# Units and sums of the feed-forward at a different offset in their slots for each pair

## The chip, the cores and the metric

The kernel runs on one core of one Trainium2 chip. The metric is the device time of one execution in microseconds; the kernel before has a median of 2101.1 us over three runs (2100.09 to 2101.67).

## What is computed

One layer of a diffusion backbone over 512 tokens of width 2048 (with 256 context tokens): a mixer, half Fourier transform and half gated linear recurrence, and then a feed-forward with a short convolution. All is in float32. The change touches the feed-forward alone, which takes more than half of the time:

```python
def conv_ffn(h, w_up, conv_w, conv_b, w_down):
    up = depthwise_conv(h @ w_up, conv_w, conv_b, FFN_CONV // 2)
    g, v = jnp.split(up, 2, axis=-1)
    return (jax.nn.gelu(g, approximate=True) * v) @ w_down

hx2 = modulate(rms_norm(x, g_ffn_pre[l]), sh2, sc2)
x = x + gt2 * rms_norm(conv_ffn(hx2, w_up[l], conv_ffn_w[l], conv_ffn_b[l], w_down[l]), g_ffn_post[l])
```

The width inside is 5632, that is 44 tiles of 128 features each for the gate g and for the value v.

## The kernel before

**Three matmuls for one product.** A float32 matrix is split into a rounded part (hi) and the rest (lo). `three` (lines 994 to 998) makes a product of 128 x 128 weights and up to 512 tokens as hi x hi (line 996), hi weights x lo data (997) and lo weights x hi data (998). Each matmul loads its own weights.

**Units.** All weights come as a stream of units of 128 x 1024 elements (`UNIT`, 8 blocks of 128 x 128). SyncE loads unit n into slot `SLOT[n]` of `w_raw` (line 471), a ring of 5 slots whose rows are `PITCH` = 1088 elements apart, so 64 elements of a slot are spare. ScalarE rounds it into the same slot of `w_hi` (lines 606 and 610); VectorE subtracts and writes `w_lo` in place of `w_raw` (lines 1536 and 1540: `twice` gives both names the same bytes). TensorE waits for `lo_done` and counts the unit as used at its last matmul; that lets SyncE load the unit four later.

**The feed-forward.** A pair is one tile of g and one of v. It has four units. In chunks of 4 pairs (`c` from 0 to 10, `p` from 0 to 3) the loops run over the pairs; after the first pair of a chunk stands the down projection of the chunk before, 8 units with 192 matmuls of 512 columns. From chunk 1 on (40 pairs) `up_pair` takes a pair in this order:
- `four_tiles` on the first unit `u`: 24 matmuls of 512 columns (8 blocks, three each);
- `seven_products` on `u + 1` and `u + 2`: the second half of the input features by a scheme with seven products instead of eight, on half the tokens. Each unit gives 8 blocks as they are and 6 blocks of sums, three matmuls each, 42 matmuls of 256 columns: 84 for both;
- `four_tiles` on the last unit `u + 3`: 24 matmuls of 512 columns.

The sums of blocks are made by VectorE (`sum_blocks`, lines 2029 to 2048) as soon as the raw unit has landed, then rounded and split as the unit is (lines 608 and 1538). `WSUM` names the units with sums: those of `u + 1` lie in the fifth slot of the ring (`SUMS0`), those of `u + 2` in `sums1_raw`, `sums1_hi` and `sums1_lo`.

**Where a block starts.** `ASIDE` = 16 elements (64 bytes): units of `WSUM` and all sums start 64 bytes into their slot (`at_slot`, `sums_of`), all other units at its first byte. Tensors named `gap_...` hold no data; they set where the next tensor begins. The streamed data are `h_hi`, `h_lo` (the input), `t_hi`, `t_lo` (sums of the input, made once) and `act_hi`, `act_lo` (the activations, for the down projection). The last four units of all (`KEPT`) are in h_hi and h_lo, without an offset.

**What sets the order.** Each engine runs its own list, written out by hand; semaphores tie them together. Nothing in the order depends on where a block lies.

Of the kernel before, what the change touches and what calls it, by code (L numbers as in the profile page):

```python
# [8 lines left out]
F32R = mybir.dt.float32r  # L9
ALU = mybir.AluOpType  # L10
ACT = mybir.ActivationFunctionType
ds = bass.ds

P = 128
# [9 lines left out]
CH = 4  # L24
NCH = FT // CH
UNIT = 8 * P
# [8 lines left out]
for _h in range(2, 8):  # L35
    _n = SLOT0 + 4 * (_h - 2)
# [10 lines left out]
UP, DOWN = {}, {}  # L47
_n = OUT_H[KT - 1][1] + 1
# [12 lines left out]
UNITS = _n + KT // 2  # L61
# [8 lines left out]
WSUM = {}  # L70
# [1 line left out]
    for _p in range(CH):  # L72
        WSUM[UP[_c, _p] + 1], WSUM[UP[_c, _p] + 2] = 0, 1
NSUM = 3 * 2 * P
ASIDE = 16

SLOT, BEFORE, TURN = [], [], []
for _n in range(UNITS):
# [3 lines left out]
SUMS0 = R0 % RING  # L82
# [85 lines left out]
def build(nc, x1_d, x_t, ctx_t, par_d, late_d, stream, ada0, adabg, gates_d, tabs_d, wf_d, out_t):  # L168
    ctx = ExitStack()
    with ctx:  # L170
# [3 lines left out]
        def sbuf(stack, name, shape, dt=F32, side=None):  # L174
            return stack.enter_context(nc.sbuf_tensor(name, shape, dt, side=side))

        def twice(stack, raw, name, shape):

            with ExitStack() as s:
                first = sbuf(s, raw, shape)  # L180
            return first, sbuf(stack, name, shape, F32R)
# [12 lines left out]
        w_raw, w_lo = twice(ctx, "w_raw", "w_lo", [P, RING, PITCH])  # L194
        w_hi = sbuf(ctx, "w_hi", [P, RING, PITCH], F32R)
# [67 lines left out]
        fin = ExitStack()  # L263
# [3 lines left out]
        t_raw, t_lo = twice(fin, "t_raw", "t_lo", [P, 4, 3 * H])  # L267
        t_hi = sbuf(fin, "t_hi", [P, 4, 3 * H], F32R)
        up_sum = sbuf(fin, "up_sum", [P, 2 * L])
        sbuf(fin, "gap_to_sums", [P, ASIDE])  # L270
        sums1_raw, sums1_lo = twice(fin, "sums1_raw", "sums1_lo", [P, NSUM])
        sbuf(fin, "gap_to_x1", [P, 256 - ASIDE])
        acc = sbuf(fin, "acc", [P, KT * L])
        with ExitStack() as s:
            late_par = sbuf(s, "late_par", [P, NLATE])
# [6 lines left out]
        mixer.close()  # L282
        with ExitStack() as s:
            sbuf(s, "late_kept", [P, NCONV])
            sbuf(s, "gap_to_sums_hi", [P, 32 + ASIDE])
            sums1_hi = sbuf(s, "sums1_hi", [P, NSUM], F32R)
            cg = sbuf(s, "cg", [P, 2, L])
            cv = sbuf(s, "cv", [P, L])
            sbuf(s, "gap_to_act", [P, 416 - 32 - ASIDE])
            act_hi = sbuf(s, "act_hi", [P, CH, L], F32R)  # L290
            act_lo = sbuf(s, "act_lo", [P, CH, L], F32R)
        ss2 = up_sum[:, 0:L]
        ss_last = up_sum[:, L:2 * L]
        fin.close()

        def at_slot(n):

            return ds(ASIDE if n in WSUM else 0, UNIT)

        def raw_unit(n):  # L300
            if n < UNITS - KEPT:
                return w_raw[:, SLOT[n], at_slot(n)]
            i = n - UNITS + KEPT
            return x0[:, 2 * i:2 * i + 2, :].rearrange("p k l -> p (k l)")

        def hi_unit(n):
            if n < UNITS - KEPT:
                return w_hi[:, SLOT[n], at_slot(n)]
            i = n - UNITS + KEPT
            return h_hi[:, 2 * i:2 * i + 2, :].rearrange("p k l -> p (k l)")  # L310

        def lo_unit(n):
            if n < UNITS - KEPT:
                return w_lo[:, SLOT[n], at_slot(n)]
            i = n - UNITS + KEPT
            return h_lo[:, 2 * i:2 * i + 2, :].rearrange("p k l -> p (k l)")

        def sums_of(n):

            if WSUM[n]:  # L320
                return sums1_raw[:, :], sums1_hi[:, :], sums1_lo[:, :]
            return tuple(w[:, SUMS0, ds(ASIDE, NSUM)] for w in (w_raw, w_hi, w_lo))

        def x1_back(k):

# [139 lines left out]
        def _(sp):  # L465
            def load_unit(n):
                if n >= UNITS - KEPT:
                    sp.wait_ge(*used(DOWN[NCH - 1] - 1))
                elif BEFORE[n] >= 0:
                    sp.wait_ge(*used(BEFORE[n]))  # L470
                sp.dma_start(raw_unit(n), stream[n]).then_inc(raw_sem(n)[0], 16)
# [125 lines left out]
        def _(act):  # L597
# [3 lines left out]
            def hi(*units):  # L601
                for n in units:
                    act.wait_ge(*raw_sem(n))
                    if n in WSUM:
                        act.wait_ge(blocks_summed, sum(u <= n for u in WSUM))
                        a.activation(hi_unit(n), raw_unit(n), ACT.Copy)  # L606
                        raw, high, _ = sums_of(n)
                        a.activation(high, raw, ACT.Copy).then_inc(hi_done, 1)
                    else:
                        a.activation(hi_unit(n), raw_unit(n), ACT.Copy).then_inc(hi_done, 1)  # L610
# [380 lines left out]
        def _(pe):  # L991
# [8 lines left out]
            def block_of(n, j):  # L1000
                return hi_unit(n)[:, P * j:P * j + P], lo_unit(n)[:, P * j:P * j + P]
# [375 lines left out]
            def seven_products(n, w, b):  # L1377

                alone_g, alone_v, common, parts = (bank[i] for i in b)
                pe.wait_ge(lo_done, n + 1)  # L1380
                _, high, low = sums_of(n)

                def product(out, block, x, start, stop):
# [144 lines left out]
        def _(dve):  # L1528
# [3 lines left out]
            def lo(*units):  # L1532
                for n in units:
                    dve.wait_ge(hi_done, n + 1)
                    if n in WSUM:
                        v.tensor_tensor(lo_unit(n), raw_unit(n), hi_unit(n).bitcast(F32), ALU.subtract)  # L1536
                        raw, high, low = sums_of(n)
                        v.tensor_tensor(low, raw, high.bitcast(F32), ALU.subtract).then_inc(lo_done, 1)
                    else:
                        v.tensor_tensor(lo_unit(n), raw_unit(n), hi_unit(n).bitcast(F32), ALU.subtract).then_inc(lo_done, 1)  # L1540
# [782 lines left out]
```

## Time and profile before

| | |
|---|---|
| median of 3 runs | 2101.1 us |
| the profiled execution | 2102.9 us |
| its span, first to last instruction | 2101.1 us |
| TensorE matmul busy | 2066.7 us, 98% |
| TensorE weight load busy | 1767.6 us |
| VectorE busy | 1529.7 us, 73% |
| ScalarE busy | 812.0 us, 39% |
| DMA, mean over the span | 148 GB/s |

Busy time of a matmul runs from its start to the end of its last column's way through the array, so matmuls that follow one another overlap in it: one of 512 columns shows 389 ns and the next starts 227 ns after it. The spacing of two starts is what a matmul costs in a full stream; it is read from the start times of the timeline.

### The profile page before, as it was taken

Reading aid. Unit: us, or ns where it says so; the run is one execution under the profiler, and the core shown is the slowest. Engines: PE = TensorE matmul, PEld = TensorE weight load, DVE = VectorE, ACT = ScalarE, POOL = GpSimd, SP = SyncE. Lnnn points to the kernel's source line nnn. Section 1 sums busy time; section 2 is a strip of 40 time slices with the busy share of each in tenths; the row PEclk is TensorE's granted clock in tenths of the full one; section 3 lists DMA queues with packets and bytes.
Section 4 is the critical chain, followed back from the end, with each engine's and each line's share of the span. In section 5 each row is a group of like instructions: output and inputs, shape, how many; then the busy total and the mean of one; then the engine's idle time right before and its main releaser. Section 6 shows DMA issues by size and latency. Waiting matters only on the chain.

```text
span 2101.1 us, 28297 instructions
## 1 busy us (share of the span) xinstructions
PE 2066.7 (98%) x11682; PEld 1767.6 (84%) x11682; DVE 1529.7 (73%) x2202; ACT 812.0 (39%) x1077; POOL 79.0 (4%) x145
## 2 busy tenths in 40 slices
PE   7999999999999999999999999999999999999998
PEld 4678887888777888888889898898988888888887
DVE  5567978876979886767767676676776768577577
ACT  5347576543323352423324243242333324233243
POOL 0000000001110000000000000000000000000002
PEclk9999999999999999999999999999999999999999
DMA  9953424434876524333333333434333333233342
GB/s 394 408 205 111 156 93 163 136 110 169 322 269 230 181 90 140 101 121 119 104 131 104 124 112 109 131 101 140 101 120 121 101 126 101 95 101 101 100 179 103
DMA packets 86193, 311.19 MB, mean 148 GB/s; under 512 B 9456, under 2 KB 13552, under 8 KB 84016
## 3 DMA queue, kind: packets, MB, share of 16 engines
q1 hardware_dynamic: 67824, 243.09, 33.3%
q0 software_dynamic: 17424, 65.50, 9.4%
q8 instruction: 92, 1.51, 0.3%
q10 hardware_dynamic: 816, 0.79, 0.1%
q14 instruction: 37, 0.30, 0.1%
HBM read 300.95 MB, written 8.39 MB: 147 GB/s over the span
## 4 chain that ended last, share of the span: by engine, by line
PE 68%; DVE 2%; DMA 1%; issue 1%; ACT 0%; DVEq 0%; ACTq 0%
PE bank L996 23%; PE bank L998 22%; PE bank L997 22%; DMA ada_raw<-in_adabg 1%; DVE w_lo L1540 1%; DVE acc L2175 0%; PE bank L1107 0%; DVE ada_acc L1572 0%; PE bank L1321 0%; DMA w_raw<-in_stream 0%; DVE x L1880 0%; DVE prod L1891 0%; ACT w_hi L610 0%; DVE ss L1548 0%; PE bank L1292 0%
## 5 line engine op out<-in xcount | busy, mean ns | idle before, releaser
L996 PE MATMUL bank<-h_hi,w_hi 128*128 128x512 f32 (+1 forms) x1968 | 711.1, 361 | 5.9 <-ACT acc L855 2.0
L997 PE MATMUL bank<-h_lo,w_hi 128*128 128x512 f32 (+1 forms) x1968 | 708.1, 360 | 0.0
L998 PE MATMUL bank<-h_hi,w_lo 128*128 128x512 f32 (+1 forms) x1968 | 706.5, 359 | 0.0
L1540 DVE TENSOR_TENSOR w_lo<-w_raw,w_hi 128x1024 fp32r<-128x1024 f32 x260 | 316.0, 1222 | 159.4 <-ACT w_hi L610 159.1
L996 PEld LDWEIGHTS bank<-h_hi,w_hi 128*128 128x128 f32 x1968 | 370.4, 188 | 65.5 <-issue 11.0
L610 ACT ACTIVATE w_hi<-w_raw 128x1024 fp32r<-128x1024 f32 x260 | 273.2, 1056 | 388.6 <-DMA w_raw<-in_stream 388.6
L998 PEld LDWEIGHTS bank<-h_hi,w_lo 128*128 128x128 f32 x1968 | 370.2, 188 | 56.8
L997 PEld LDWEIGHTS bank<-h_lo,w_hi 128*128 128x128 f32 x1968 | 372.8, 189 | 49.0
L996 PE MATMUL bank<-act_hi,w_hi 128*128 128x512 f32 (+1 forms) x688 | 265.0, 385 | 1.9 <-DVE acc L2147 1.5
L997 PE MATMUL bank<-act_lo,w_hi 128*128 128x512 f32 (+1 forms) x688 | 264.3, 384 | 0.0
L998 PE MATMUL bank<-act_hi,w_lo 128*128 128x512 f32 (+1 forms) x688 | 264.2, 384 | 0.0
L606 ACT ACTIVATE w_hi<-w_raw 128x1024 fp32r<-128x1024 f32 x80 | 85.0, 1062 | 335.9 <-DVE w_raw L2048 335.9
L2075 DVE TENSOR_TENSOR acc<-acc,bank 128x512 f32<-128x512 f32 x144 | 98.3, 687 | 134.6 <-PE bank L998 134.4
L996 PEld LDWEIGHTS bank<-act_hi,w_hi 128*128 128x128 f32 x688 | 129.2, 188 | 28.1 <-DVE h_lo L1540 1.9
L997 PEld LDWEIGHTS bank<-act_lo,w_hi 128*128 128x128 f32 x688 | 129.3, 188 | 25.7
L998 PEld LDWEIGHTS bank<-act_hi,w_lo 128*128 128x128 f32 x688 | 129.3, 188 | 25.6
L1572 DVE SCALAR_TENSOR_TENSOR ada_acc<-ada_raw,csil,ada_acc 128x1024 f32<-128x1024 f32 x105 | 134.5, 1281 | 10.8 <-DMA ada_raw<-in_adabg 6.5
L558 POOL DMA_DIRECT2D ada_raw<-in_adabg x112 | 59.8, 534 | 1537.3 <-DVE ada_acc L1572 1135.2
L1536 DVE TENSOR_TENSOR w_lo<-w_raw,w_hi 128x1024 fp32r<-128x1024 f32 x80 | 97.4, 1217 | 0.0
L996 PE MATMUL bank<-t_hi,w_hi 128*128 128x256 f32 x320 | 89.9, 281 | 0.0
L997 PE MATMUL bank<-t_lo,w_hi 128*128 128x256 f32 x320 | 89.9, 281 | 0.0
L998 PE MATMUL bank<-t_hi,w_lo 128*128 128x256 f32 x320 | 89.9, 281 | 0.0
(340 smaller groups left out, 2707.8 us busy)
## 6 DMA issues: line engine op xcount, KB each, us to landing
w_raw<-in_stream SPq DMA_DIRECT2D x340, 512.0 KB, 3.5
ada_raw<-in_adabg POOLq DMA_DIRECT2D x112, 512.0 KB, 4.7
ada_raw<-in_ada SPq DMA_DIRECT2D x64, 512.0 KB, 13.6
x<-in_x_t SPq DMA_DIRECT2D x4, 1024.0 KB, 8.4
acc<-in_adabg SPq DMA_DIRECT2D x8, 512.0 KB, 6.3
x<-in_x_t POOLq DMA_DIRECT2D x4, 1024.0 KB, 9.0
x_kept_d<-x SPq DMA_DIRECT2D x4, 1024.0 KB, 5.6
c<-in_ctx_t SPq DMA_DIRECT2D x2, 1024.0 KB, 14.1
```

Of the source, the lines that this page charges most:

```text
L558: pool.dma_start(ada_raw(slot), adabg[COLS[q // KT] * KT + q % KT]).then_inc(ada_in[slot], 16)
L606: a.activation(hi_unit(n), raw_unit(n), ACT.Copy)
L610: a.activation(hi_unit(n), raw_unit(n), ACT.Copy).then_inc(hi_done, 1)
L996: t.matmul(out, w, v, start=start, stop=False)
L997: t.matmul(out, w, v_l, start=False, stop=False)
L998: return t.matmul(out, w_l, v, start=False, stop=stop)
L1536: v.tensor_tensor(lo_unit(n), raw_unit(n), hi_unit(n).bitcast(F32), ALU.subtract)
L1540: v.tensor_tensor(lo_unit(n), raw_unit(n), hi_unit(n).bitcast(F32), ALU.subtract).then_inc(lo_done, 1)
L1572: v.scalar_tensor_tensor(dst, ada_raw(s), scale, dst, ALU.mult, ALU.add).then_inc(ada_eaten, 1)
L2075: v.tensor_tensor(tile(acc, m), tile(acc, m), bank[4 + m % 4][:, :], ALU.add).then_inc(down_added, 1)
```

## The change

It makes the offset a table by unit, with one entry for the hi copy (`HI_ASIDE`) and one for the raw and lo copies (`LO_ASIDE`), in elements of 4 bytes. Pairs are counted from chunk 1 on (`_n` from 0 to 39). The first unit, the two middle units and their sums get another offset in each pair; the last unit, the down projection and everything ahead of chunk 1 stay at 0. In bytes, with s = 16 x (`_n` mod 16):

| pairs | first unit hi, lo | middle units and sums hi, lo |
|---|---|---|
| 0 to 15 | s, s | s, s |
| 16 to 31 | 0, s | 64, s |
| 32 to 39 | 2s + 8, 2s + 8 | 0, 2s + 16 |

The tensors for the second sums grow by 64 elements and the gaps beside them shrink, so that all else stays where it was.

```diff
-ASIDE = 16
+HI_ASIDE, LO_ASIDE = [0] * UNITS, [0] * UNITS
+for _c in range(1, NCH):
+    for _p in range(CH):
+        _n, _u = (_c - 1) * CH + _p, UP[_c, _p]
+        _step = 4 * (_n % 16)
+        if _n < 16:
+            _first, _seven = (_step, _step), (_step, _step)
+        elif _n < 32:
+            _first, _seven = (0, _step), (16, _step)
+        else:
+            _first, _seven = (2 * _step + 2, 2 * _step + 2), (0, 2 * _step + 4)
+        HI_ASIDE[_u], LO_ASIDE[_u] = _first
+        for _i in (1, 2):
+            HI_ASIDE[_u + _i], LO_ASIDE[_u + _i] = _seven
...
-        sbuf(fin, "gap_to_sums", [P, ASIDE])
-        sums1_raw, sums1_lo = twice(fin, "sums1_raw", "sums1_lo", [P, NSUM])
-        sbuf(fin, "gap_to_x1", [P, 256 - ASIDE])
+        sums1_raw, sums1_lo = twice(fin, "sums1_raw", "sums1_lo", [P, NSUM + 64])
+        sbuf(fin, "gap_to_x1", [P, 256 - 64])
...
-            sbuf(s, "gap_to_sums_hi", [P, 32 + ASIDE])
-            sums1_hi = sbuf(s, "sums1_hi", [P, NSUM], F32R)
+            sbuf(s, "gap_to_sums_hi", [P, 32])
+            sums1_hi = sbuf(s, "sums1_hi", [P, NSUM + 64], F32R)
...
-            sbuf(s, "gap_to_act", [P, 416 - 32 - ASIDE])
+            sbuf(s, "gap_to_act", [P, 416 - 32 - 64])
...
-        def at_slot(n):
-
-            return ds(ASIDE if n in WSUM else 0, UNIT)
-
...
-                return w_raw[:, SLOT[n], at_slot(n)]
+                return w_raw[:, SLOT[n], ds(LO_ASIDE[n], UNIT)]
...
-                return w_hi[:, SLOT[n], at_slot(n)]
+                return w_hi[:, SLOT[n], ds(HI_ASIDE[n], UNIT)]
...
-                return w_lo[:, SLOT[n], at_slot(n)]
+                return w_lo[:, SLOT[n], ds(LO_ASIDE[n], UNIT)]
...
+            high, low = ds(HI_ASIDE[n], NSUM), ds(LO_ASIDE[n], NSUM)
             if WSUM[n]:
-                return sums1_raw[:, :], sums1_hi[:, :], sums1_lo[:, :]
-            return tuple(w[:, SUMS0, ds(ASIDE, NSUM)] for w in (w_raw, w_hi, w_lo))
+                return sums1_raw[:, low], sums1_hi[:, high], sums1_lo[:, low]
+            return w_raw[:, SUMS0, low], w_hi[:, SUMS0, high], w_lo[:, SUMS0, low]
```

## Rows read from the trace of the kernel before

**Rows 1.** The page: busy time, share, instructions; granted clock by slice.
```profile
PE 2066.7 (98%) x11682; PEld 1767.6 (84%) x11682; DVE 1529.7 (73%) x2202; ACT 812.0 (39%) x1077; POOL 79.0 (4%) x145
...
PEclk9999999999999999999999999999999999999999
```

**Rows 2.** The page: the chain that ended last, by engine and by line.
```profile
PE 68%; DVE 2%; DMA 1%; issue 1%; ACT 0%; DVEq 0%; ACTq 0%
PE bank L996 23%; PE bank L998 22%; PE bank L997 22%; DMA ada_raw<-in_adabg 1%; DVE w_lo L1540 1%; DVE acc L2175 0%; PE bank L1107 0%; DVE ada_acc L1572 0%; PE bank L1321 0%; DMA w_raw<-in_stream 0%; DVE x L1880 0%; DVE prod L1891 0%; ACT w_hi L610 0%; DVE ss L1548 0%; PE bank L1292 0%
```

**Rows 3.** Waits of PE, 905 to 2060 us: total us, times, longest.
```profile
PE bank L996 <- DVE acc L2147: 1.9, 3, 0.9
PE bank L996 <- DVE act_lo L1988: 0.4, 1, 0.4
```

**Rows 4.** Timeline of PE, one pair: start us, duration us; first unit, then middle.
```profile
1356.46 0.39 PE L996 MATMUL bank<-h_hi,w_hi 128*128 128x512 f32 x1
...
1361.67 0.39 PE L998 MATMUL bank<-h_hi,w_lo 128*128 128x512 f32 x1
1361.89 0.28 PE L996 MATMUL bank<-h_hi,w_hi 128*128 128x256 f32 x1
```

**Rows 5.** The same timeline: last middle matmul, then the last unit.
```profile
1371.67 0.28 PE L998 MATMUL bank<-t_hi,sums_lo 128*128 128x256 f32 x1
1371.79 0.40 PE L996 MATMUL bank<-h_hi,w_hi 128*128 128x512 f32 x1
...
1372.49 0.40 PE L996 MATMUL bank<-h_hi,w_hi 128*128 128x512 f32 x1
...
1373.18 0.39 PE L996 MATMUL bank<-h_hi,w_hi 128*128 128x512 f32 x1
...
1377.26 0.39 PE L996 MATMUL bank<-h_hi,w_hi 128*128 128x512 f32 x1
```

**Rows 6.** Timeline of PE, last down projection, weights from h_hi and h_lo.
```profile
2071.78 0.28 PE L996 MATMUL bank<-act_hi,h_hi 128*128 128x256 f32 x1
...
2072.74 0.28 PE L998 MATMUL bank<-act_hi,h_lo 128*128 128x256 f32 x1
```

**Rows 7.** Timeline of PE, Fourier stage, weights from eo_hi and eo_lo.
```profile
417.87 0.29 PE L998 MATMUL bank<-m_hi,eo_lo 128*128 128x256 f32 x1
...
419.06 0.28 PE L996 MATMUL bank<-m_hi,eo_hi 128*128 128x256 f32 x1
```

**Rows 8.** Timeline of PE, mixer: 256 columns after 512, and 512 after 256.
```profile
179.02 0.28 PE L996 MATMUL bank<-hc_hi,w_hi 128*128 128x256 f32 x1
179.13 0.28 PE L997 MATMUL bank<-hc_lo,w_hi 128*128 128x256 f32 x1
...
179.37 0.40 PE L996 MATMUL bank<-xc_hi,g_hi 128*128 128x512 f32 x1
...
180.07 0.40 PE L996 MATMUL bank<-xc_hi,g_hi 128*128 128x512 f32 x1
```

**Rows 9.** Groups of VectorE, 905 to 2060 us: count, busy us, mean ns, idle before.
```profile
L1540 DVE TENSOR_TENSOR w_lo<-w_raw,w_hi 128x1024 fp32r<-128x1024 f32 x145 | 177.4, 1223 | 117.0 <-ACT w_hi L610 116.9
L1536 DVE TENSOR_TENSOR w_lo<-w_raw,w_hi 128x1024 fp32r<-128x1024 f32 x70 | 85.2, 1217 | 0.0
```

**Rows 10.** Timeline, all engines: a first middle unit made ready, and its first matmul.
```profile
1082.97 0.95 DVE L1538 TENSOR_TENSOR w_lo<-w_raw,w_hi 128x768 fp32r<-128x768 f32 x1
...
1085.81 0.28 PE L996 MATMUL bank<-h_hi,w_hi 128*128 128x256 f32 x1
```

**Rows 11.** Loads of units, 1000 to 2000 us: least, median, longest.
```profile
DMA to landing us min/median/max: 3.3/3.5/5.9
```

**Rows 12.** Waits of VectorE for a landed unit, 1000 to 2000 us: total, times, longest.
```profile
DVE w_raw L2043 <- DMA w_raw<-in_stream: 17.6, 13, 2.3
```

## The prediction

> **What bounds the kernel now.** I read four views in this order. First the page's busy times and its slices: the matmul array is busy 2066.7 of 2101.1 us, VectorE 1529.7 and ScalarE 812.0, with the granted clock of its slices at nine tenths or more throughout [rows 1]. Then the chain that ended last: 67 of its 68 percentage points on PE are the three matmul lines 996 to 998 [rows 2]. Then the waits of PE over the feed-forward (905 to 2060 us): 2.3 us in all, most of it in the last down projection [rows 3]. So within the pairs no weight unit is late, and the kernel is as long as the sum of the spacings from one matmul start to the next. What the change can move directly is that spacing; everything else works only by making a unit late.
>
> The reader is to see that the spacing is not the columns alone. In the first unit of a pair 24 matmuls of 512 columns start in 5.43 us, 226 to 227 ns each [rows 4]; in the two middle units 84 of 256 columns start from 1361.89 to 1371.79 us, 117.8 ns each [rows 4, 5]. In the last down projection, where matmuls of 256 columns take weights from h_hi and h_lo with no offset, eight start in 0.96 us, 120.0 ns each [rows 6]. The gap tensors of lines 215 to 291 and the slot pitch put every tensor that the feed-forward's matmuls stream, and every slot that they load, at one remainder of 128 bytes (worked out from the sizes in the allocations). So 120.0 ns belongs to an offset of 0, 117.8 to one of 64 bytes. A third point: in the Fourier stage moving data (m_hi, m_lo) and weights (eo_hi, eo_lo) are 32 bytes apart by the same count, and ten spacings take 417.87 to 419.06 us, 119.0 ns each [rows 7]. The offset of the weights against the streamed data therefore costs or gives about 2 ns a matmul, and these three points are all that the trace has.
>
> For 512 columns there is only offset 0. But there is the return to it: of the first six matmuls of the last unit, after the 84, three take 0.70 us (1371.79 to 1372.49, 233 ns each) and three 0.69 (to 1373.18, 230 ns), and only then do 18 of them take 4.08 us (to 1377.26, 226.7 ns each) [rows 5]. The even 227 is a state that the stream settles into, and off it the array is slower here.
>
> **The change, part by part.** No instruction is added, removed or moved, and no wait. What changes is the start of a block in its slot. Of 40 pairs from the second chunk on:
> - The first unit (24 matmuls of 512 columns) leaves offset 0 by a remainder of 128 bytes in 14 of the first 16 pairs, for w_lo alone in 14 of the next 16, and by 8 bytes and more in the last 8: 36 pairs.
> - The middle units and sums (84 of 256) leave 64 bytes. In the first 16 pairs both copies walk in steps of 16 bytes: 2 pairs at 64, 2 at 0, 12 between. In the next 16 w_hi stays at 64 and w_lo walks: 14 pairs. In the last 8 w_hi is at 0 and w_lo between.
> - The last unit and the down projection stay at 0.
>
> *Middle units.* An offset of 0 costs 120.0 - 117.8 = 2.2 ns, one between 119.0 - 117.8 = 1.2 ns (the Fourier point, the nearest row). First 16 pairs: 84 x (2 x 2.2 + 12 x 1.2) = 1.6 us. Next 16: one load in three is moved; I take half of 1.2, since the three share one stream: 84 x 14 x 0.6 = 0.7 us. Last 8: two loads at 0 and one between, 1.9 ns: 84 x 8 x 1.9 = 1.3 us. Sum 3.6 us. Bounds: single spacings of 0.11 us occur, but as the first of 256 columns after three of 512 (179.02 to 179.13 us), repaid by three of 512 in 0.70 us right after (179.37 to 180.07) [rows 8]; no row holds under 117.8. For the end below I take 1.2 ns gained, the same size as the loss between: 36 x 84 x 1.2 = 3.6 us off. For the end above, 2.2 ns everywhere: 6.7 us.
>
> *First unit.* If an offset keeps the stream from its settled state, 230.0 - 226.7 = 3.3 ns, the second three above; 36 x 24 x 3.3 = 2.9 us. Ends: 2.2 ns gained, as 64 bytes gives in the middle units, 1.9 us off; and 6.6 ns lost, the first three's 233.3, 5.7 us.
>
> *Crossings.* Each pair now pays 1.39 - 6 x 0.2267 = 0.03 us once on returning to the last unit [rows 5]. New crossings stand where a shifted first unit follows the last one; I take half of that, 36 x 0.015 = 0.5 us, with 0 and 1.0 as ends.
>
> *Off the path.* DMAs, ScalarE's roundings and VectorE's subtractions now write and read at 16 or 8 bytes. VectorE already does it at two offsets: 1223 ns at 0 (line 1540) and 1217 at 64 bytes (line 1536) [rows 9]; 6 ns by 160 instructions is 1 us of an engine with 570 us to spare. The cover is the lead of the units: the tightest is the first middle unit, whose w_lo is ready at 1082.97 + 0.95 = 1083.92 us and first used at 1085.81 [rows 10], 1.9 us early. Unit loads land 3.3 to 5.9 us after issue, median 3.5 [rows 11]. So I cost all this at nothing; below nothing is excluded, as no wait of PE is there to shorten.
>
> Sum: 3.6 + 2.9 + 0.5 = 7.0 us. The profiled execution took 2102.9 us with a span of 2101.1, against a median of 2101.1; the terms are differences, so they go on the median: 2101.1 + 7.0 = 2108.1 us.
>
> **A rule that speaks against this working.** The rows show 120.0 and 117.8 ns for the same 256 columns [rows 4 to 6]. The Trainium skill (SBUF — State Buffer, Who interferes with whom) gives TensorE two independent read ports, one for streamed data and one for weights, and says that it never waits on anyone; by that an offset could cost nothing, and the trace does not agree, unless the 2.2 ns comes from something else that differs in the tail. This is the second rival. The same page (its box on cachelines) has lines of 16 bytes; by that only the first units of the last 8 pairs, which start 8 bytes into a line, would differ.
>
> **Rivals.**
> 1. *Slower, by late units.* A load whose rows begin on a 16-byte or 8-byte multiple may land later. For it: sum_blocks already waits for landings [rows 12]; against: both offsets of before land alike, but both are multiples of 32 bytes within one 64. The point from which it decides is 1.9 us more per landing, over half of the median 3.5. If landings doubled, the first middle unit would be 3.5 - 1.9 = 1.6 us late in the 24 pairs whose raw block starts off a multiple of 32 bytes: 38 us at worst, and with half of them 19: about 2120. The Trainium skill (Collectives: The Full Stack, Rules for kernel authors) asks for 32-byte alignment to prevent a read-modify-write; no run here shows one.
> 2. *No change, by independence.* The middle units' 117.8 against 120.0 is due to act_hi as moving data or to h_hi as weights, not to 64 bytes; or each stream settles at the same spacing whatever the offset, only shifted in time. For it: streams of offset 0 do return to 227 from any start within six matmuls. Against: the Fourier point between the two. Price: 0 to 2 us, 2101 to 2103.
> 3. *Slower at the upper ends.* 6.7 + 5.7 + 1.0 = 13.4 us: 2114.5. Beyond it, should the untried offsets be as much worse than 0 as 0 is worse than 64 bytes, another 6.7 us: 2121.
> 4. *Faster, by the lower ends.* The conflict is smallest somewhere between: 3.6 + 1.9 = 5.5 us off, 2095.6. For it: 0 was never the best where another was seen. Against: the 64 bytes of now is the best of three points.
>
> **How the numbers follow.** Forecast (offsets cost about what the three points say, 2105 to 2112) 0.45; rival 2, 0.27; rival 3, 0.12; rival 4, 0.12; rival 1, 0.04. A measurement of this kernel can tell about 0.2% (4.2 us) from no change, so "slower" begins at 2105.3: nearly all of the forecast less 0.02, rivals 3 and 1, together 0.59. "Same": rival 2 and 0.02 of the forecast, with 0.02 of rival 4: 0.31. "Faster": 0.10. The range leaves out rival 1, half of rival 3 above 2115 and most of rival 4 below 2098: 2098 to 2115.
>
> **What would show it.** In the trace of after: spacings of the 84 middle matmuls pair by pair, 117.8 in the pairs whose offset is 64 or 192 bytes and 119 to 120 elsewhere; spacings of the first unit above 227 in 36 pairs; the last unit still with its 0.03 us; PE's waits still near 2 us. It is wrong if first units stay at 227 at any offset (rival 2), if a row of an offset lies far off 117 to 120, or if PE waits for VectorE at line 996 (rival 1).

## The result and the profile after

The changed kernel takes 2106.5 us (median of 10 runs) beside 2101.5 for the kernel before (10 runs on the same chip): 1.0021 times as long over all runs, 95% interval 1.0013 to 1.0029: a small loss, clear of no change. The forecast was 2108.1 us, with a range of 2098 to 2115. The profiled execution has a span of 2105.8 us, 4.7 more than before.

The waits and the engines other than TensorE are as they were; the matmul array is busy 7 us more, and recorded busy times overlap. First a line of the page of the changed kernel (busy time, share, instructions), then the waits of PE from 905 to 2065 us, then what the loads of units took to land from 900 to 2060 us (least, median, longest):

```profile
PE 2073.7 (98%) x11682; PEld 1769.5 (84%) x11682; DVE 1530.1 (73%) x2202; ACT 811.9 (39%) x1077; POOL 78.7 (4%) x145
```

```profile
PE bank L1005 <- DVE acc L2156: 1.9, 3, 0.8
PE bank L1005 <- DVE act_lo L1997: 0.3, 1, 0.3
```

```profile
DMA to landing us min/median/max: 3.3/3.5/5.6
```

PE waits 2.2 us where it waited 2.3 [rows 3], the loads land in 3.5 us in the median, as in [rows 11], and the 66 of the 215 that begin off a multiple of 32 bytes do so too (3.3 us at least, 5.0 at most), and VectorE's time is 0.4 us more. So the 4.7 us lie in the spacings of the matmuls. Summed from one start to the next over all 40 pairs, first units take 4.1 us more, middle units 0.4, last units 0.2, the down projections nothing: 4.7 (4.65 before rounding).

The timeline of PE shows where (start us, duration us; each time the first matmul of a unit). Pair 1, first unit at 16 bytes, 24 matmuls from 827.25 us on; pair 2, at 32 bytes, from 848.10 on:

```profile
827.25 0.39 PE L1005 MATMUL bank<-h_hi,w_hi 128*128 128x512 f32 x1
...
832.69 0.28 PE L1005 MATMUL bank<-h_hi,w_hi 128*128 128x256 f32 x1
...
848.10 0.39 PE L1005 MATMUL bank<-h_hi,w_hi 128*128 128x512 f32 x1
...
853.69 0.28 PE L1005 MATMUL bank<-h_hi,w_hi 128*128 128x256 f32 x1
```

5.44 us are 226.7 ns a matmul, as at 0 bytes in [rows 4]; 5.59 us are 232.9. (The lines are rounded to 0.01 us, which is 0.4 ns a matmul here; the table below is made from the unrounded starts.) Then the 84 middle matmuls of pair 4 and of pair 20. Both have them at 64 bytes in both copies, as all pairs had before:

```profile
895.75 0.28 PE L1005 MATMUL bank<-h_hi,w_hi 128*128 128x256 f32 x1
...
905.65 0.40 PE L1005 MATMUL bank<-h_hi,w_hi 128*128 128x512 f32 x1
...
1406.64 0.28 PE L1005 MATMUL bank<-h_hi,w_hi 128*128 128x256 f32 x1
...
1416.16 0.40 PE L1005 MATMUL bank<-h_hi,w_hi 128*128 128x512 f32 x1
```

9.90 us are 117.8 ns a matmul, 9.52 us are 113.3. The same offsets, the same work, two speeds: nothing in the prediction has room for this. By the table of offsets the two pairs differ in the first unit ahead, at (64, 64) in pair 4 and (0, 64) in pair 20.

Since each pair of the changed kernel has its own offsets, its trace can be laid out as a table, each value seen once and behind its own neighbours. Mean spacing in ns over the unit, from the start times of the timeline (offsets in bytes, hi and lo copy; s as in the table of the change):

| s | first unit (s, s) | first unit (0, s) | middle (s, s) | middle (64, s) |
|---|---|---|---|---|
| 0 | 226.7 | 226.7 | 119.9 | 117.8 |
| 16 | 226.7 | 226.7 | 118.3 | 117.8 |
| 32 | 233.1 | 233.1 | 118.4 | 117.8 |
| 48 | 233.3 | 231.9 | 118.3 | 116.7 |
| 64 | 233.3 | 230.9 | 117.8 | 113.4 |
| 80 | 231.9 | 231.5 | 118.8 | 117.8 |
| 96 | 234.2 | 232.1 | 118.7 | 118.8 |
| 112 | 233.3 | 233.0 | 119.9 | 118.6 |
| 128 | 232.7 | 231.1 | 118.8 | 118.2 |
| 144 | 226.7 | 226.7 | 119.8 | 117.8 |
| 160 | 233.3 | 233.0 | 119.9 | 117.9 |
| 176 | 230.0 | 230.8 | 118.1 | 117.0 |
| 192 | 228.9 | 231.1 | 117.8 | 113.6 |
| 208 | 231.8 | 230.8 | 116.6 | 117.8 |
| 224 | 233.3 | 231.4 | 116.6 | 117.0 |
| 240 | 226.7 | 226.7 | 117.3 | 117.7 |

In the last eight pairs the first units (8 to 232 bytes in steps of 32) run at 226.7 to 233.7 ns, with 226.7 at 40 bytes, the middle ones at 117.8 to 118.9. So first units know one good rhythm, 226.7 ns, which they have at 0, 16, 40, 144 and 240 bytes, and else run 2 to 8 ns above it, never below. The two middle streams at 113.4 and 113.6 ns have one rhythm, three spacings of 113, 113 and 114 ns over and over, 113.3 in the mean; the rest is the first one or four spacings, which are longer.

### The profile page after: what moved, and what is told of

It reads as the page before. It is cut to its first block, busy times and chain, and to the rows that moved or that the text cites. A ratio compares the mean times of both kernels' runs of the same rounds, so it can differ in the third digit from the quotient of the medians.

```text
span 2105.8 us, 28297 instructions
## 1 busy us (share of the span) xinstructions
PE 2073.7 (98%) x11682; PEld 1769.5 (84%) x11682; DVE 1530.1 (73%) x2202; ACT 811.9 (39%) x1077; POOL 78.7 (4%) x145
## 4 chain that ended last, share of the span: by engine, by line
PE 69%; DVE 2%; DMA 1%; issue 0%; ACT 0%; DVEq 0%; ACTq 0%
PE bank L1005 23%; PE bank L1007 23%; PE bank L1006 23%; DMA ada_raw<-in_adabg 0%; DVE acc L2184 0%; DVE w_lo L1549 0%; PE bank L1116 0%; PE bank L1325 0%; DMA w_raw<-in_stream 0%; ACT h_hi L619 0%; DVE ada_acc L1581 0%; DVE x L1889 0%; PE bank L1330 0%; PE bank L1301 0%; DVE acc L2156 0%
## 5 line engine op out<-in xcount | busy, mean ns | idle before, releaser
L1545 DVE TENSOR_TENSOR w_lo<-w_raw,w_hi 128x1024 fp32r<-128x1024 f32 x80 | 97.5, 1219 | 0.0
```

## The experiments

Two theories stood against each other. **H**: a stream of matmuls settles into a rhythm, and which one depends on the offsets and on the state in which the stream is entered. **F**: each offset has a price of its own. Each experiment keeps all instructions of the changed kernel and alters only the table of offsets, unless its edit says more. In the edits `...` stands for lines left out, `OFFSETS` lists for each pair the bytes of the first unit (hi, lo) and of the middle units (hi, lo), and `HI_ASIDE` and `LO_ASIDE` count elements of 4 bytes (16 is 64 bytes, 48 is 192).

**First units alone.** The offsets of the changed kernel for first units, 64 bytes for all middle units and sums.

```diff
+OFFSETS = (
+    (0, 0, 64, 64), (16, 16, 64, 64), (32, 32, 64, 64), (48, 48, 64, 64),
...
-        HI_ASIDE[_u], LO_ASIDE[_u] = _first
...
+        _fh, _fl, _sh, _sl = (_x // 4 for _x in OFFSETS[(_c - 1) * CH + _p])
+        HI_ASIDE[_u], LO_ASIDE[_u] = _fh, _fl
...
-            HI_ASIDE[_u + _i], LO_ASIDE[_u + _i] = _seven
+            HI_ASIDE[_u + _i], LO_ASIDE[_u + _i] = _sh, _sl
```

> The first units' offsets of the changed kernel in all 40 pairs, the middle units and sums at 64 bytes as before. Theory H (a stream of matmuls settles into a rhythm, and which one depends on how it is entered as well as on the offset): first units add the 4.1 us that the changed trace shows for them, and pair 20 (first unit 0 and 64 bytes) runs its 84 middle matmuls at 113.4 ns as it did there; the middle units together lose nothing or gain 0.4 us or more; in all 3.3 to 4.1 us slower. Rival F (each offset has one price of its own): first units plus 4.1 us, middle units 117.8 ns in every pair, in all 4.1 us slower.

Measured: 2100.6 us beside 2102.1, ratio 0.9993 (0.9983 to 1.0003), no change that the runs can tell. In the trace first units cost 4.07 us more than before, as forecast, and middle units 5.13 us less, which neither theory had: with all middle units at (64, 64), 26 pairs run them at 117.8 ns and 14 pairs at 113.3 to 113.6, those whose first unit is at (128, 128), (160, 160), (176, 176), (0, 32), (0, 64), (0, 80), (0, 96), (0, 112), (0, 128), (0, 176), (0, 224), (104, 104), (136, 136) or (200, 200). The recorded durations go with the spacings, 276 ns where the stream has 113.3 and 281 where it has 117.8; they are no second witness, as the end of a matmul is modelled in the profile. Least, median and longest of the matmuls on the second sums, 905 to 2060 us (before they are all 281 ns):

```profile
L1012 PE MATMUL bank<-t_lo,sums_hi x142: 276/281/281, 904.8 to 2027.1; 128*128 128x256 f32 x142
```

Equal offsets, two rhythms and nothing between: F falls. H had the mechanism and not its reach; it named pair 20 alone, and its 3.3 to 4.1 us slower stand against 1.1 us less in the spacings.

**Middle units alone.** First units at 0, middle units and sums as in the changed kernel.

```diff
+OFFSETS = (
+    (0, 0, 0, 0), (0, 0, 16, 16), (0, 0, 32, 32), (0, 0, 48, 48),
...
-        HI_ASIDE[_u], LO_ASIDE[_u] = _first
...
+        HI_ASIDE[_u], LO_ASIDE[_u] = _fh, _fl
```

> The middle units' and sums' offsets of the changed kernel, the first units at 0 as before. Theory H: pairs 20 and 28 (64, 64 and 64, 192 bytes), which ran at 113.4 and 113.6 ns in the changed kernel, fall to about 117.8 when entered from a first unit at 0, so the middle units cost 0.4 + 0.7 = 1.1 us. Rival F: they keep the changed kernel's spacings, pair 20 at 113.4 too, 0.4 us in all.

Measured: 2104.1 us beside 2102.1, ratio 1.0006 (0.9996 to 1.0015), no change that the runs can tell. The trace gives middle units 0.92 us more than before. Pair 20, at (64, 64), and pair 28, at (64, 192), timeline of PE:

```profile
1406.02 0.28 PE L1011 MATMUL bank<-h_hi,w_hi 128*128 128x256 f32 x1
...
1415.91 0.40 PE L1011 MATMUL bank<-h_hi,w_hi 128*128 128x512 f32 x1
...
1659.60 0.28 PE L1011 MATMUL bank<-h_hi,w_hi 128*128 128x256 f32 x1
...
1669.13 0.40 PE L1011 MATMUL bank<-h_hi,w_hi 128*128 128x512 f32 x1
```

Pair 20 has fallen back to 117.7 ns (117.8 from the unrounded starts), as H expects; pair 28 has not, 113.5 ns. So (64, 64) depends on the entry, and (64, 192) may not. Other values of the table hang on the entry too: behind a first unit at 0, (96, 96) runs at 117.4 ns where the changed kernel had 118.7, and (128, 128) at 120.1 where it had 118.8.

**Every pair as pair 20.**

```diff
+        HI_ASIDE[_u], LO_ASIDE[_u] = 0, 16
...
+            HI_ASIDE[_u + _i], LO_ASIDE[_u + _i] = 16, 16
```

> Every pair as pair 20 of the changed kernel: first unit 0 (hi) and 64 (lo) bytes, middle units and sums 64 and 64. Theory H: 84 x (117.8 - 113.4) = 0.37 us gained and 24 x (231.0 - 226.7) = 0.10 us lost in each pair, 40 x 0.27 = 10.7 us faster than before, about 2090.7. Rival F (the offsets 64 and 64 are worth 117.8, as before, and pair 20 was a single occurrence): 4.1 us slower, about 2105.5.

Measured: 2093.0 us beside 2102.1, ratio 0.9956 (0.9939 to 0.9974), that is 9.2 us faster. In the trace middle units take 14.7 us less than before and first units 4.1 more, 10.6 us in all, against 10.7 expected. One pair, first unit, middle units and the first matmul of the last unit:

```profile
888.55 0.39 PE L998 MATMUL bank<-h_hi,w_hi 128*128 128x512 f32 x1
...
894.10 0.28 PE L998 MATMUL bank<-h_hi,w_hi 128*128 128x256 f32 x1
...
903.62 0.40 PE L998 MATMUL bank<-h_hi,w_hi 128*128 128x512 f32 x1
```

5.55 us instead of 5.43, 9.52 instead of 9.90. All 40 pairs show these times within 0.01 us, though VectorE is busy in 28% of the middle units' time in one pair and in 85% in another, and ScalarE in 11% to 47%: the work beside it does not set the spacing. Middle units keep the offset of before here, so all that they gain comes from what stands ahead of them.

**Twenty entries, two kinds of middle units.** Pairs 0 to 19 at (64, 64), pairs 20 to 39 at (64, 192), each behind the same 20 first units.

```diff
+OFFSETS = (
+    (0, 0, 64, 64), (16, 16, 64, 64), (144, 144, 64, 64), (240, 240, 64, 64),
...
+        HI_ASIDE[_u], LO_ASIDE[_u] = _fh, _fl
...
+            HI_ASIDE[_u + _i], LO_ASIDE[_u + _i] = _sh, _sl
```

> One look at 20 different first units (both copies from 0, 16, 40, 64, 144, 192, 240 bytes), each followed by middle units at 64, 64 (pairs 0 to 19) and at 64, 192 bytes (pairs 20 to 39). Theory H: among equal middle units some run at 117.8 and some at 113.4 to 113.6 ns, with (0, 64) in pair 17 and (0, 192) in pair 38 at about 113.5; where a first unit keeps 226.7 ns and the middle ones run at 113.5, 0.36 us a pair are to be had for nothing. Rival F: all of pairs 0 to 19 alike, all of 20 to 39 alike, within 0.2 ns.

Measured, a single execution (2097.1 us), so only its trace is read: at (64, 64) only the entry from (0, 64) leads to 113.4 ns. The 17 first units that themselves keep 226.7 ns, such as (16, 16), (40, 40) or (144, 240), all lead to 117.8, and so do (0, 192) and (64, 0). At (64, 192) all 20 entries lead to 113.4 to 113.6 ns over the 84, that is to the rhythm of 113.3 after one to five spacings, also those from a first unit at 0 (pair 20 of this kernel):

```profile
1404.37 0.28 PE L1011 MATMUL bank<-h_hi,w_hi 128*128 128x256 f32 x1
...
1413.91 0.40 PE L1011 MATMUL bank<-h_hi,w_hi 128*128 128x512 f32 x1
```

9.54 us, 0.36 less than in [rows 4, 5], and the first unit loses nothing.

**All middle units at 64 and 192 bytes.** First units at 0.

```diff
+        HI_ASIDE[_u], LO_ASIDE[_u] = 0, 0
...
+            HI_ASIDE[_u + _i], LO_ASIDE[_u + _i] = 16, 48
```

> First units at 0 as before; middle units and sums with the hi copy at 64 and the lo copy at 192 bytes in all 40 pairs. Theory H (a stream settles into a rhythm; at 64, 192 all 20 entries tried led to 113.3 ns, at 64, 64 only some): 84 x (117.8 - 113.3) less the first matmuls = 0.353 us in each pair, 14.1 us faster than before, about 2088. Rival G (the trace's spacings overstate: what the middle units gain comes back later, since the profiled span of a kernel moved less than its spacings say): at most half of it, 7 us.

Measured: 2088.7 us beside 2101.8, ratio 0.9937 (0.9924 to 0.9950), 13.2 us faster than the kernel before, and with that below both kernels. The trace has middle units at 14.1 us less, and first units, last units and down projections within 0.04 us of before. G, which allowed 7 us at most, falls: the interval is 10.5 to 16 us, so what the spacings say arrives in the time. The matmuls on the second sums, 905 to 2045 us, where before has 281 throughout:

```profile
L998 PE MATMUL bank<-t_hi,sums_hi x140: 276/276/276, 965.3 to 2013.7; 128*128 128x256 f32 x140
L999 PE MATMUL bank<-t_lo,sums_hi x140: 276/276/276, 965.4 to 2013.8; 128*128 128x256 f32 x140
```

**Forty offsets for matmuls of 512 columns.** First units with hi and lo copies apart, middle units at (64, 192).

```diff
+OFFSETS = (
+    (64, 16, 64, 192), (64, 32, 64, 192), (64, 96, 64, 192), (64, 128, 64, 192),
...
+        HI_ASIDE[_u], LO_ASIDE[_u] = _fh, _fl
...
+            HI_ASIDE[_u + _i], LO_ASIDE[_u + _i] = _sh, _sl
```

> One look at 40 offsets of the first unit (hi and lo copies apart: 64,16 64,32 64,96 64,128 64,160 64,192 64,224; 128 with 0,32,64,96,192,240; 192 with 0,32,64,128,224; 32 with 0,64,96,128,160,224; 96 with 0,32,64,160,224; 160 with 0,32,96; 224 with 0,32,96,160; 48,0 112,0 16,64 144,192), middle units at 64, 192 throughout. If matmuls of 512 columns have a better rhythm than 226.7 ns as those of 256 had a better one than 117.8, some pair shows it: 222 ns or so. If 226.7 is their best (the 45 offsets seen so far give 226.7 or 229 to 234), none lies below 226.6; the middle units run at 113.3 in all pairs either way.

Measured, a single execution (2094.5 us): first units run at 228.9 ns, at (192, 0), to 234.3, at (96, 32); none reaches 226.7. Middle units run at 113.3 to 113.6 ns in 26 pairs and at 113.7 to 114.0 in 14; all 40 reach the rhythm of 113.3, after at most 10 spacings. PE's waits stay at 2.1 us. Among some 90 offsets there is none better than 0 for 512 columns.

**Both sides moved.** The activations that the down projection streams and its weights get an offset by chunk; `tokens` is a new helper that slices act_hi and act_lo at the chunk's offset. First units at 0, middle units at 64 bytes. ScalarE's rounding and VectorE's subtraction write through `tokens` too.

```diff
+DATA_AT, WEIGHTS_AT = (0, 32, 0, 32, 64, 0, 64, 96, 16, 128, 0), (0, 0, 32, 32, 0, 64, 64, 96, 64, 128, 0)
+for _c in range(NCH):
+    for _i in range(KT // 2):
+        HI_ASIDE[DOWN[_c] + _i] = LO_ASIDE[DOWN[_c] + _i] = WEIGHTS_AT[_c] // 4
...
+        def tokens(t, c, k, a=0, b=L):
+            return t[:, ds(DATA_AT[c] // 4 + k * L + a, b - a)]
...
-                        mm = three(bank[4 + m % 4][:, :], *block_of(n, CH * (m % 2) + k), act_hi[:, k, :], act_lo[:, k, :],
+                        mm = three(bank[4 + m % 4][:, :], *block_of(n, CH * (m % 2) + k), tokens(act_hi, c, k), tokens(act_lo, c, k),
```

> Down projections of chunks 0 to 9 with the streamed activations and the weights at offsets (data, weights) in bytes: (0,0) (32,0) (0,32) (32,32) (64,0) (0,64) (64,64) (96,96) (16,64) (128,128); all else as before. If the distance between streamed data and weights is what counts, (32,32), (64,64), (96,96) and (128,128) keep 226.7 ns a matmul, and (0,32) and (0,64) show 233 as the first units at 32 and 64 did, (32,0), (64,0) and (16,64) something above 226.7. If the weights' own place counts, (32,32), (64,64) and (96,96) show 233 as well and (32,0) and (64,0) keep 226.7.

Measured, a single execution (2105.9 us). First and last of the 192 matmuls of a down projection, at (data, weights) of (32, 0), (0, 32), (32, 32) and (64, 64):

```profile
906.94 0.40 PE L1007 MATMUL bank<-act_hi,w_hi 128*128 128x512 f32 x1
...
951.50 0.40 PE L1009 MATMUL bank<-act_hi,w_lo 128*128 128x512 f32 x1
...
1034.98 0.39 PE L1007 MATMUL bank<-act_hi,w_hi 128*128 128x512 f32 x1
...
1079.55 0.40 PE L1009 MATMUL bank<-act_hi,w_lo 128*128 128x512 f32 x1
...
1162.99 0.39 PE L1007 MATMUL bank<-act_hi,w_hi 128*128 128x512 f32 x1
...
1206.31 0.40 PE L1009 MATMUL bank<-act_hi,w_lo 128*128 128x512 f32 x1
...
1546.79 0.39 PE L1007 MATMUL bank<-act_hi,w_hi 128*128 128x512 f32 x1
...
1590.12 0.39 PE L1009 MATMUL bank<-act_hi,w_lo 128*128 128x512 f32 x1
```

Over 191 spacings: 233.3, 233.3, 226.8 and 226.9 ns. (96, 96) and (128, 128) give 226.9 and 226.7, (0, 64) 233.3, (64, 0) 228.9 and (16, 64) 234.6, the last two without the first spacing, which is long in their chunks in the kernel before as well (324 ns). Moving one side by 32 bytes costs 6.7 ns whichever side it is, and moving both takes it back. What counts is the distance from streamed data to weights, with its sign: +64 and -64 bytes differ by 4.4 ns. It seems to count modulo 256 bytes: -64 and -32 have 228.9 and 233.3 ns, the same as first units at (192, 192) and (224, 224) in the changed kernel. The place of either is free at the four places tried with both moved; (16, 64), 48 bytes apart, has 234.6 where first units at (48, 48) had 233.3, so that it is free at every place is not shown.

## Why the prediction was right, and where not

**What bounds the kernel: right.** PE waits 2.2 us where it waited 2.3, and 4.7 us of spacings are 4.7 us of span.

**First unit: right in kind, too small.** Forecast 2.9 us at 3.3 ns a matmul, measured 4.1, crossings into it included; 31 pairs leave 226.7 ns, and in them it is 5.5 ns (31 x 24 x 5.5 = 4.1). The term was taken from the second three matmuls after the middle units, and the first three, 6.6 ns, were the end above; the truth lies between. That 226.7 is a state that the stream settles into, and that no other offset is faster, holds for all that were tried. But seven of the 36 pairs counted as moved kept it: those at 16, 144 and 240, with both copies or the lo copy alone, and that at 40.

**Remainders of 128 bytes: wrong.** The prediction took 128 for 0 and 192 for 64. First units at 128 run at 232.7 ns, at 0 at 226.7, and middle units behind a first unit at 0 run at 117.8 ns at (64, 64) and 113.6 at (64, 192). (192, 192) did give 117.8, as (64, 64) did in pair 4. Streams that move together by 128 do not show it (226.7 above), so the count fails for the distance; the experiment on both sides speaks for 256. The Fourier point was misplaced by the same count: by the allocations of the kernel before, eo_hi and eo_lo begin 224 bytes past a multiple of 256 and m_hi and m_lo 128, so the weights stand 96 bytes after the data, and (96, 96) in the changed kernel runs at 118.7 ns where that point had 119.0.

**Middle units: wrong in size.** Forecast 3.6 us, measured 0.4. The price between, taken as 1.2 ns, is 0.6 in the mean of the 12 pairs of the first 16 that it was meant for, from 1.1 ns gained at 208 and 224 bytes to 2.1 lost at 112 and 160; the first 16 pairs together took 0.90 us, where 1.6 was forecast. The next 16 gained 0.75, where a loss of 0.7 was forecast. Two things were missed. Some pairs run under 117.8: 116.6 at 208 and 224 bytes, 116.7 at (64, 48), and the two at 113.4 and 113.6 alone give 0.7 us back. And the last eight pairs, at 0 for the hi copy, pay 0.2 us, not 1.3. The step that failed is the one from "no row holds under 117.8", which is true of the trace of before, to a price for each offset: three points were read as a curve with its best at the one in use. By the prediction's own list a row far off 117 to 120 ns was to count against it, and 113.4 and 113.6 are such rows. Whether the single spacing of 113 ns in [rows 8] has to do with the rhythm of 113.3 is not shown: spacings of 119 and 120 follow it.

**Crossings: small, and in part not told apart.** The last units take 0.2 us more in all, so the return keeps its 0.03 us a pair. What it costs to cross from a last unit into a shifted first one, the 0.5 us of the forecast, lies in the 4.1 us of the first units.

**Off the path: right.** The lead of 1.9 us was not touched, since no load lands later (at most 5.6 us, 5.9 before); rival 1, the late units, fell with it. VectorE takes 1216 to 1224 ns for a middle unit's lo copy where it took 1217.

**The sum** was 7.0 us for 4.7 in the trace and 5.0 between the medians: first units and crossings together 0.7 us short (3.4 forecast, 4.1 measured), the last units 0.2 us that no term held, middle units 3.2 us over. The sign rests on the term that was short. That the total came out near is in part luck: the largest term was nine times too large, a term that was too small made up for some of it, and the faster rhythm showed in only two pairs; the same 40 first units with all middle units left at 64 bytes made no loss at all. Rival 4, faster by the lower ends, was a real possibility with the wrong reason: a faster rhythm exists, at the offset already in use behind another entry, and at (64, 192). Rival 2 had a true half: streams do return to a rhythm, but not at every offset.

**The rule on ports.** The last experiment shows that moving either operand by 32 bytes turns 226.7 into 233.3 ns, and moving both takes it back. The Trainium skill (SBUF — State Buffer, Who interferes with whom) gives TensorE two independent read ports and says that it never waits on anyone; these runs disagree as far as its own two operands go, by 6.7 ns a matmul at 32 bytes, while the spacing does not follow how busy VectorE and ScalarE are (9.52 to 9.53 us in all 40 pairs above). That only starts off a multiple of 16 bytes would differ, which the prediction weighed too, is not so either: a first unit at 32 bytes goes to 233.1 ns, and one at 40 bytes keeps 226.7. The Trainium skill's 32-byte alignment of buffers (Collectives: The Full Stack, Rules for kernel authors) stands among rules for collectives; these loads do not need it: 3.3, 3.5 and 5.6 us to landing, and 5.0 at most for those off 32 bytes.

**Still open.** Why these distances and not others, what in the chip holds the state, and whether 512 columns have a better rhythm at distances that were not tried. That the entry decides is shown by equal middle units behind unequal first ones; what of the entry decides is not: first units at (0, 192) and (0, 64) both leave 226.7, and only the second leads (64, 64) to 113.3.

## What to carry to other kernels

Where TensorE is busy throughout and no wait is left, read the spacing of matmul starts, not the busy time: 117.8 and 113.6 ns for the same 256 columns were 14 us of 2101. Its lever is the distance in bytes between streamed data and weights, for each copy apart, and a table of offsets by iteration in one kernel measures 40 of them in one run. Read such a table with care, as each iteration also changes what the next one is entered from. Take an offset whose rhythm does not depend on what runs ahead, as (64, 192) here, and confirm it with the whole kernel.

## What the runs showed of the hardware that was not expected

- A stream of weight load and matmul has more than one steady spacing at the same offsets. 256 columns at (64, 64): 117.8 ns, or 113.3 after none to four longer spacings, held to the end of the 84 matmuls and chosen by what ran ahead; nothing between in the 100 pairs that ran so in three experiments.
- For 512 columns 226.7 ns is the best of some 90 offsets and is held at 0, 16, 40, 144 and 240 bytes; elsewhere the mean lies at 229 to 235.
- What counts is the distance from the streamed data to the weights, with its sign: 226.7 ns at 0, 233.3 at +32, -32 and +64 bytes, 228.9 at -64, and 226.7 to 226.9 where both move by the same 32 to 128 bytes.
- Offsets of 8 and 16 bytes cost neither the loads (3.5 us to landing) nor VectorE (1219 ns) anything.
